# A hybrid encoder step on one core: x rows added by VectorE on the way out of PSUM, and another order of the second projections

## The chip, the cores and the metric

One core of a Trainium2 chip runs the whole program. The metric is the device time of one execution in microseconds (us); a smaller number is better. A GB/s is 10^9 bytes a second, a KB in the tables of the profile is 1024 bytes.

## The reference

One layer, with the same weights for 1024 new frames (prompt) and 32 frames of a running stream (sample), D_MODEL = 1024, float32 throughout:

```
x += concat[mLSTM(4 heads of 128), sliding-window attention(8 heads of 64)](rmsnorm(x) W_in) W_out     # W_in: 1024 x 2824
h  = rmsnorm(x)
q  = h W_q;  s1, s2 = q halves x two sets of 128 sub-keys        # 8 heads
top 16 of s1, of s2, then top 16 of their 256 sums -> 16 of 16384 experts per head and row
x += sum over 8 heads x 16 experts of  softmax(top) * gelu(u[idx] . h) * v[idx]     # u, v: rows of 1024 float32
y  = rmsnorm(x)
```

It also returns the last 128 keys and values and the final mLSTM state of both groups. Each row of x reads 128 rows of u and 128 of v, gathered by index from HBM.

## The kernel before

**Tiles and groups.** The 1056 rows are nine tiles: 0 to 7 are the prompt's, of 128 rows, and tile 8 (`SAMPLE`) has 32. Mixing a tile (projection, mLSTM, attention, output projection, norm, queries, key scores) needs the tiles before it. The expert part goes by subtiles of 32 rows: 33 subtiles q, two groups g = 2q and 2q + 1 each, 66 groups of 16 slots, so 1056 slots t = 16 g + k. A group handles 32 rows x 4 heads = 128 partitions at once, and a slot is one of their 16 experts: a u row and a v row for each partition, 512 KB each. GpSimd issues the two indirect gathers of a slot in turn (`gather_u` of the next group, `gather_v` of this one) into rings of 5 and 7 buffers. VectorE forms the dot product of u with h (L1141) and, in `weigh` (L1109), the matrix of weights of a group; TensorE multiplies the weights by the v rows (L1502) and so sums heads and experts of a subtile in the PSUM tile `acc`. Even experts go to the subtile's own 32 partitions of `acc`, odd ones to 32 others.

**Out of PSUM.** At the start of a subtile `begin_parts` (TensorE, L1462) puts the subtile's x rows into its own part of `acc`, by a product with the identity. When its 32 slots are done, `gather_parts` on ScalarE copies the other part to SBUF (L733), TensorE adds that to the own part (L1448), and ScalarE copies the own part to `xt` (L736). After the last subtile of a tile it sums the squares (L742), and `finish` on VectorE scales the rows (L1119), from where they are stored.

**What sets the order.** Every engine runs the same loop over slots, each a program of its own, in order. The mixing of tile m is woven in by the tables `PE_AT`, `ACT_AT` and `DVE_AT`: a step's name, a part and a row r, and `slot_of(m, r)` turns a row into a slot. Tiles 5 to 7 take 1.24 slots a row, tile 4 0.60, tile 3 0.60 in its second part, and the sample tile 1.06. The slot says only where in each engine's stream the step stands; semaphores do the rest, and a step that waits holds up its engine. In the tables `out_proj` (L1382) ends at row 61; `residual` (VectorE, L1028) adds its sum to x, `norm_root` (ScalarE) and `normalise` (VectorE) follow, then `h2_transpose`, sixteen `query` steps (L1397) and four `score_keys` (L1408).

**Two passes of the projection.** The weights W_in, W_out and W_q don't fit in SBUF together: W_in (six chunks of columns) shares its place `weights` with W_out and W_q. Tiles 0 to 3 (`FIRST` = 4) are projected at the start. At slot 288 (`AGAIN`) W_in comes again, and tiles 4, 5, 6, 7 and the sample are projected at slots 288 to 391: 24 slots a tile, a half chunk every second slot (`project_at`), 8 for the sample. Each chunk is scaled on its way out of PSUM to `po_again` (L581, L834, and L849 for the sample's last two) and stored to a scratch tensor in HBM (L390, L401). Then W_out (L375) and W_q in four loads of two row blocks (L366) come back. `load_p` (L333 to L336) reads a tile's rows of the projection (644, 256 and 512 KB) and of the rotation table (8 KB) before its mixing. The queue of SyncE issues all of this, in the order of its program. For tile 4 the first steps that need the rows are `gates` on VectorE (L894) and `qk_transpose` on TensorE (L1288), at slot 399.

```
def begin_parts(q):
    if q >= 2: pe.wait_ge(sub_out, q - 1)
    for half in range(2):
        T.matmul(acc[r, cols], ident[r, r], xt[m % 2][r, cols], start=True, stop=False)
```

## Time and profile before

| | |
|---|---|
| median of 3 runs | 3286.49 us (3281.36 to 3294.59) |
| the profiled execution | 3287.95 us |
| its span, first to last instruction | 3286.2 us |
| mean granted clock of TensorE | 0.84 |
| DMA | 1206.27 MB, 367 GB/s over the span |
| busy: TensorE, VectorE, GpSimd, ScalarE | 2585.3, 2079.2, 1995.7, 580.3 us |

The DMA share of a stretch is the mean busy share of the core's sixteen DMA engines; it can come out a little over 1. Records of TensorE count twice for each float32 product that the code writes: a product of 512 columns is two records. A stretch of the trace is named by its us from the start of the span.

### The profile page before, as it was taken

The numbers are of one execution on the slowest core, as the hardware profiler recorded it, in microseconds if no ns is written. First come the engines' busy times: TensorE is split into PE (matmuls) and PEld (weight loads), VectorE is DVE, ScalarE is ACT, GpSimd is POOL, SyncE is SP. The second block draws the span as 40 slices with busy tenths as digits, with TensorE's granted clock in tenths as the row PEclk, the third lists the DMA queues.
The fourth block names the chain that finished last, engine by engine and source line by source line (L and its number), as shares of the span: only waits on it lengthen the run. The fifth ranks groups of instructions, "written<-read, shape, count | busy, mean of one in ns | idle before, by whom it ended". The sixth has DMA issues, their size and how long they took to land.

```text
span 3286.2 us, 34549 instructions
## 1 busy us (share of the span) xinstructions
PE 2585.3 (79%) x11351; PEld 1055.1 (32%) x11351; DVE 2079.2 (63%) x5202; ACT 580.3 (18%) x1057; POOL 1995.7 (61%) x2128
## 2 busy tenths in 40 slices
PE   8995886788769899947967786778767886789666
PEld 4562352235224433313522242234222341125111
DVE  1246677776776467637657776777677667765653
ACT  2211111211121212112112111211122111210111
POOL 0015576767765466636567676777676676755775
PEclk9996897789788999968888897789878887775878
DMA  6079999999999999998899999999999999988998
GB/s 243 26 267 403 344 376 405 396 364 407 409 386 379 344 407 407 373 384 316 330 361 408 396 401 407 399 398 403 407 409 384 366 407 399 406 337 296 394 405 331
DMA packets 351818, 1206.27 MB, mean 367 GB/s; under 512 B 37840, under 2 KB 55128, under 8 KB 349592
## 3 DMA queue, kind: packets, MB, share of 16 engines
q0 software_dynamic: 304128, 1107.43, 86.3%
q1 hardware_dynamic: 47512, 96.64, 7.9%
q8 instruction: 91, 1.49, 0.2%
q14 instruction: 87, 0.71, 0.1%
HBM read 1188.42 MB, written 15.60 MB: 366 GB/s over the span
## 4 chain that ended last, share of the span: by engine, by line
PE 40%; DMA 23%; DVE 13%; POOL 10%; issue 6%; DVEq 4%; ACT 2%; SPq 1%; ACTq 1%; POOLq 0%
DMA ring<-in_peer_u_dram,idx 13%; PE acc L1502 12%; DMA ring<-in_peer_v_dram,idx 7%; DVE ring L1141 7%; PE mx L1397 6%; POOL ring L529 5%; POOL ring L518 5%; PE mx L1382 4%; PE acc L1213 4%; PE acc L1462 3%; PE mx L1228 3%; DVEq L1045 2%; PE h2p L1437 2%; PE acc L1448 2%; DMA proj_scratch<-weights 1%
## 5 line engine op out<-in xcount | busy, mean ns | idle before, releaser
L1502 PE MATMUL acc<-ring,wk 128*32 128x512 f32 x4224 | 1259.6, 729 | 474.8 <-DMA ring<-in_peer_v_dram,idx 436.1
L1141 DVE SCALAR_TENSOR_TENSOR ring<-ring,h2p 128x1024 f32<-128x1024 f32 x1056 | 1281.0, 1216 | 556.1 <-DMA ring<-in_peer_u_dram,idx 466.5
L518 POOL DMA_INDIRECT ring<-in_peer_u_dram,idx x1056 | 997.1, 944 | 720.5 <-DVE ring L1141 264.9
L529 POOL DMA_INDIRECT ring<-in_peer_v_dram,idx x1056 | 996.5, 944 | 550.8 <-issue 273.6
L1502 PEld LDWEIGHTS acc<-ring,wk 128*32 128x32 f32 x4224 | 252.5, 123 | 1305.6 <-issue 1233.1
L1397 PEld LDWEIGHTS mx<-reg,weights 128*128 128x128 f32 x2048 | 249.9, 202 | 73.5 <-issue 73.5
L1397 PE MATMUL mx<-reg,weights 128*128 128x128 f32 (+1 forms) x2048 | 263.7, 288 | 2.0 <-DVEq L1024 1.3
L1462 PE MATMUL acc<-xt,ident 32*32 32x512 f32 x132 | 100.1, 899 | 94.1 <-DVEq L1110 94.1
L721 ACT ACTIVATE gl<-dots 128x16 f32<-128x16 f32 x66 | 14.2, 216 | 702.7 <-DVEq L1144 702.6
L1437 PE MATMUL h2p<-ch,ident 32*32 32x512 f32 x528 | 86.3, 780 | 55.6 <-DVEq L1144 55.6
L1382 PE MATMUL mx<-weights,reg 128*128 128x512 f32 (+1 forms) x256 | 128.2, 655 | 0.0
L736 ACT COPY xt<-acc 32x1024 f32<-32x1024 f32 x33 | 33.1, 1003 | 377.0 <-PE acc L1448 377.0
L1228 PE MATMUL mx<-weights,reg 128*128 128x512 f32 (+1 forms) x192 | 85.2, 588 | 3.2 <-ACTq L569 3.2
L1141 DVE DVE_READ_ACCUMULATOR ring<-ring,h2p 128x1 f32 x1056 | 87.2, 83 | 0.0
L681 ACT COPY pj<-mx 128x512 f32<-128x512 f32 (+1 forms) x36 | 19.8, 550 | 374.7 <-PE mx L1397 374.6
L721 ACT ACT_TABLE_LOAD x66 | 84.7, 1283 | 5.6
L1228 PE MATMUL mx<-weights 128*128 128x512 f32 (+1 forms) x192 | 83.8, 580 | 0.0
L1213 PE MATMUL acc<-weights,ring 128*128 128x512 f32 (+1 forms) x192 | 79.4, 572 | 0.0
L1213 PE MATMUL acc<-weights 128*128 128x512 f32 (+1 forms) x192 | 77.5, 559 | 0.0
L1448 PE MATMUL acc<-part,ident 32*32 32x512 f32 x132 | 74.6, 690 | 1.1 <-ACTq L734 1.1
L1028 DVE TENSOR_TENSOR xt<-xt,mx 128x1024 f32<-128x1024 f32 (+1 forms) x9 | 11.0, 1220 | 100.1 <-PE mx L1382 100.1
L1382 PEld LDWEIGHTS mx<-weights,reg 128*128 128x128 f32 (+1 forms) x256 | 48.8, 197 | 74.3 <-issue 73.9
(279 smaller groups left out, 2339.6 us busy)
## 6 DMA issues: line engine op xcount, KB each, us to landing
weights<-in_w_in_dram SPq DMA_DIRECT2D x10, 2048.0 KB, 18.9
ring<-in_peer_u_dram,idx POOLq DMA_INDIRECT x1056, 8.1
ring<-in_peer_v_dram,idx POOLq DMA_INDIRECT x1056, 8.0
weights<-in_peer_w_q_dram SPq DMA_DIRECT2D x8, 2048.0 KB, 26.9
ring<-in_peer_w_q_dram SPq DMA_DIRECT2D x8, 1024.0 KB, 5.7
weights<-in_w_out_dram SPq DMA_DIRECT2D x2, 4096.0 KB, 23.5
proj_scratch<-weights SPq DMA_DIRECT2D x20, 256.0 KB, 6.1
pj<-proj_scratch SPq DMA_DIRECT2D x7, 644.0 KB, 13.9
```

Source lines behind the costliest of these rows:

```text
L518: pool.indirect_dma_start(ring[:, n % NU, :], None, u_d, bass.IndirectOffsetOnAxis(ap=idx[:, g % 4, k:k + 1], axis=0)).then_inc(u_in[n % N ...
L529: pool.indirect_dma_start(ring[:, NU + n % NV, :], None, v_d, bass.IndirectOffsetOnAxis(ap=idx[:, g % 4, k:k + 1], axis=0)).then_inc(v_in[ ...
L721: S.activation(gl[:, :], dots[:, g % 2, :], ACT.Gelu)
L1141: V.scalar_tensor_tensor(ring[:, n % NU, :], ring[:, n % NU, :], 1.0, h2p[:, :], ALU.mult, ALU.mult, accum_out=dots[:, (g + 1) % 2, k:k + ...
L1213: last = T.matmul(pbank[c], hT1[b][:, k, :], win_s[c][:, k, :], start=k == 0, stop=k == DC - 1)
L1228: last = T.matmul(pbank_again[c], hT1_again[b][:, k, :], win_s[c][:, k, :], start=k == 0, stop=k == DC - 1)
L1382: last = T.matmul(mx[0:n, 2 + half, :], t8[:, k, 0:n], w, start=k == 0, stop=k == DC - 1)
L1397: last = T.matmul(mx[:, i // 4, i % 4 * P:i % 4 * P + n], w, t8[:, k, 0:n], start=k == 0, stop=k == DC - 1)
L1437: last = T.matmul(h2p[j * SUB:(j + 1) * SUB, cols], ident[r, r], ch[m % 2][r, cols], start=True, stop=True)
L1448: last = T.matmul(acc[r, cols], ident[other, other], part[other, cols], start=False, stop=True)
L1462: T.matmul(acc[r, cols], ident[r, r], xt[m % 2][r, cols], start=True, stop=False)
L1502: last = T.matmul(acc[j:j + SUB, cols], wk[:, g % 2, i, :], ring[:, NU + (TOPK * g + i) % NV, cols], start=not own and g % 2 == 0 and i == ...
```

## The change

There are two parts.

**The x rows.** `begin_parts` no longer issues products. The first even expert of a subtile starts the sum in its own part (`start` for i < 2). ScalarE's `gather_parts` ends after the copy of the other part. A new step on VectorE, `add_rows`, stands at k = 6 of every even group, waits for TensorE's sum and adds the own part of `acc` to `xt`. The squares of a finished tile move into `square_rows` on ScalarE, at k = 7 of every eighth group. VectorE's last `finish` but one moves from k = 5 to k = 14 of its group.

**The order of the second projections.** `ORDER` makes it 5, 6, 7, sample, 4, in the same slots 288 to 391. Tile 4, which is mixed next, is scaled from PSUM straight to where the mixing reads it (`first`), as tile 0 is, and is neither stored nor read back; `load_p(4)` reads the rotation table alone. The sample's stores now stand ahead of the weights, and W_out and the four loads of W_q are issued one by one, each when a chunk of tile 4 is done. The tables change too: `residual` and what follows up to `h2_copy` start three rows later (`residual` 63 to 66), the queries two (73 to 75), the scores one (90 to 91), tile 4's slots begin six earlier (396 to 390), and tile 3's second part takes 0.56 slots a row.

```
+ORDER = [0, 1, 2, 3, 5, 6, 7, SAMPLE, FIRST]
+AT_S, AT_LAST = TILES - 2, TILES - 1
...
-PE_AT += [("out_proj", i, 58 + i // 2) for i in range(8)] + [("h2_transpose", 0, 69)]
-PE_AT += [("query", i, 73 + i) for i in range(16)] + [("score_keys", i, 90 + i) for i in range(4)]
+PE_AT += [("out_proj", i, 58 + i // 2) for i in range(8)] + [("h2_transpose", 0, 72)]
+PE_AT += [("query", i, 75 + i) for i in range(16)] + [("score_keys", i, 91 + i) for i in range(4)]
...
-        return 206 + r * 85 // 100 if r < 51 else 262 + (r - 51) * 60 // 100
+        return 206 + r * 85 // 100 if r < 51 else 263 + (r - 51) * 56 // 100
     if m == 4:
-        return 396 + r * 60 // 100
+        return 390 + r * 60 // 100
...
+    return AGAIN + 2 * (((n - FIRST) * NC_ + c) * 2 + half) - (2 * 2 * (NC_ - 2) if n == AT_LAST else 0)
...
             def load_p(m):
                 sp.wait_ge(keys_scored, m)
-                if m == FIRST:
-                    sp.wait_ge(sc_ready, m)
...
+                if m == FIRST:
+                    sp.dma_start(rot[0:n, :], rot_tab[r:r + n, :]).then_inc(p_in, 16)
+                    return
...
+                load_x1_again(AT_LAST)
+                sp.wait_ge(chunk_act, copies_until(AT_S) + 1)
...
+                for c in range(1, NC_):
+                    sp.wait_ge(chunk_ready, chunks_until(AT_LAST) + c + 1)
+                    if c == 1:
+                        load_wout()
+                    else:
+                        if c == NC_ - 1:
+                            sp.wait_ge(po_out, 16 * NC_ * (TILES - 1 - FIRST))
+                        load_wq(2 * (c - 2))
...
+                if m == AT_LAST:
+                    V.tensor_scalar(first[c], pbank_again[c], rinv, None, ALU.mult)
...
                 act.drain().then_inc(part_ready, 1)
-                act.wait_ge(sub_ready, q + 1)
-                S.copy(xt[m % 2][r, :], acc[r, :])
-                act.drain().then_inc(sub_out, 1)
...
+            def add_rows(q):
+                m, s = q // 4, q % 4
+                r = slice(s * SUB, (s + 1) * SUB)
+                dve.wait_ge(sub_ready, q + 1)
+                V.tensor_tensor(xt[m % 2][r, :], xt[m % 2][r, :], acc[r, :], ALU.add)
+                dve.drain().then_inc(sub_out, 1)
...
             def begin_parts(q):
-                for half in range(2):
-                    cols = slice(half * 512, half * 512 + 512)
-                    T.matmul(acc[r, cols], ident[r, r], xt[m % 2][r, cols], start=True, stop=False)
...
-                                                start=not own and g % 2 == 0 and i == 1, stop=not own and g % 2 == 1 and i == TOPK - 1)
+                                                start=g % 2 == 0 and i < 2, stop=not own and g % 2 == 1 and i == TOPK - 1)
```

SyncE's queue, where the second projections end and tile 4's rows are loaded (`reg` holds x rows that are projected, `weights` holds both the weights and `po_again`). Before:

```order
L390 DMA proj_scratch<-weights 128x264 [waits chunk_dve]
L375 DMA weights<-in_w_out_dram 128x8x1024 [waits chunk_ready]
L366 DMA weights<-in_peer_w_q_dram 128x2x2048 x2
L401 DMA proj_scratch<-weights 32x512 [waits chunk_act]
L401 DMA proj_scratch<-weights 32x512 x3
L366 DMA weights<-in_peer_w_q_dram 128x2x2048 [waits chunk_dve]
L401 DMA proj_scratch<-weights 32x512
L401 DMA proj_scratch<-weights 32x264
L366 DMA weights<-in_peer_w_q_dram 128x2x2048 [waits po_out]
L333 DMA pj<-proj_scratch 128x1024 [waits sc_ready,keys_scored]
L334 DMA vx<-proj_scratch 128x4x128
L335 DMA pj<-proj_scratch 128x1288
```

The same place in the changed kernel:

```order
L410 DMA proj_scratch<-weights 128x264 [waits chunk_dve]
L342 DMA reg<-in_x_prompt_dram 128x1024 [waits rms1_ready,h1_transposed]
L417 DMA proj_scratch<-weights 32x512 [waits chunk_act]
L417 DMA proj_scratch<-weights 32x512 x3
L417 DMA proj_scratch<-weights 32x512 [waits chunk_dve]
L417 DMA proj_scratch<-weights 32x264
L395 DMA weights<-in_w_out_dram 128x8x1024 [waits chunk_ready]
L386 DMA weights<-in_peer_w_q_dram 128x2x2048 [waits chunk_ready] x3
L386 DMA weights<-in_peer_w_q_dram 128x2x2048 [waits po_out,chunk_ready]
L351 DMA rot<-in_rotation_dram 128x16 [waits keys_scored]
```

The sample's six stores have moved ahead of W_out and W_q, the three reads of tile 4's projection are gone, and the rotation table stands directly behind the last load of W_q.

VectorE at slot 422 of the changed kernel, in the middle of tile 4's mixing (L1184 is the dot product of a slot, L1162 is `finish` of tile 2, L1115 a step of the top 16):

```order
L1160 RECIPROCAL yr<-yr 128x1
L1162 SCALAR_TENSOR_TENSOR xt<-xt,yr,mx 128x1024
L1184 SCALAR_TENSOR_TENSOR ring,dots<-ring,h2p 128x1024
L1152 TENSOR_TENSOR xt<-xt,acc 32x1024
L1115 MAX top<-co 128x8
L1184 SCALAR_TENSOR_TENSOR ring,dots<-ring,h2p 128x1024
```

The row L1152 is new, one for each of the 33 subtiles; the others stood in VectorE's stream before.

## Rows read from the trace of the kernel before

**Rows 1.** The page, part 1: busy time, share of the span, instructions
```profile
PE 2585.3 (79%) x11351; PEld 1055.1 (32%) x11351; DVE 2079.2 (63%) x5202; ACT 580.3 (18%) x1057; POOL 1995.7 (61%) x2128
```

**Rows 2.** The page, part 3, GpSimd's gathers: packets, MB, share of sixteen engines' span
```profile
q0 software_dynamic: 304128, 1107.43, 86.3%
```

**Rows 3.** Stretches: length, busy us of each engine, granted clock, DMA share, GB/s
```profile
271.40:3286.20 3014.80, 2341.78 (x10271) 911.49 (x10270) 1999.22 (x4963) 520.09 (x937) 1966.00 (x2083) 0.83 0.98 382
...
1396.50:1482.00 85.50, 37.70 (x159) 9.61 (x160) 28.21 (x68) 12.54 (x17) 29.69 (x32) 0.66 0.95 376
1482.00:1526.00 44.00, 31.46 (x135) 13.21 (x135) 39.98 (x120) 11.17 (x27) 30.82 (x33) 0.81 0.98 372
1526.00:1690.80 164.80, 138.85 (x773) 73.56 (x772) 92.65 (x217) 27.45 (x50) 89.28 (x95) 0.85 0.84 314
...
1593.90:1647.00 53.10, 49.53 (x335) 34.26 (x334) 40.38 (x97) 9.25 (x14) 31.06 (x33) 0.94 0.88 327
...
2501.30:2592.80 91.50, 74.36 (x273) 29.05 (x272) 61.92 (x145) 19.44 (x40) 57.61 (x62) 0.82 0.94 360
2887.20:3050.10 162.90, 148.91 (x620) 71.89 (x621) 92.86 (x227) 16.86 (x28) 89.07 (x95) 0.69 0.83 308
...
3050.10:3135.50 85.40, 50.78 (x160) 10.24 (x159) 57.53 (x142) 9.68 (x15) 64.66 (x69) 0.79 1.03 409
3254.00:3286.20 32.20, 17.18 (x68) 3.96 (x68) 1.42 (x2) 4.73 (x6) 9.87 (x11) 0.91 0.57 210
```

**Rows 4.** Groups by line: busy us, mean ns | idle before, what ended it
```profile
L1397 PE MATMUL mx<-reg,weights 128*128 128x128 f32 (+1 forms) x2048 | 263.7, 288 | 2.0 <-DVEq L1024 1.3 <-issue 0.8
L1462 PE MATMUL acc<-xt,ident 32*32 32x512 f32 x132 | 100.1, 899 | 94.1 <-DVEq L1110 94.1
...
L736 ACT COPY xt<-acc 32x1024 f32<-32x1024 f32 x33 | 33.1, 1003 | 377.0 <-PE acc L1448 377.0
...
L1028 DVE TENSOR_TENSOR xt<-xt,mx 128x1024 f32<-128x1024 f32 (+1 forms) x9 | 11.0, 1220 | 100.1 <-PE mx L1382 100.1
```

**Rows 5.** DMA issues by line: count, KB each, median us to landing
```profile
weights<-in_peer_w_q_dram SPq DMA_DIRECT2D x8, 2048.0 KB, 26.9
...
pj<-proj_scratch SPq DMA_DIRECT2D x7, 644.0 KB, 13.9
...
pj<-proj_scratch SPq DMA_DIRECT2D x7, 512.0 KB, 6.5
...
reg<-in_x_prompt_dram SPq DMA_DIRECT2D x4, 512.0 KB, 9.9
vx<-proj_scratch SPq DMA_DIRECT2D x7, 256.0 KB, 11.6
```

**Rows 6.** Waits from 1404 to 1482 us: us in total, times, longest
```profile
DVE weights L849 <- DMA proj_scratch<-weights: 33.2, 1, 33.2
...
DVE g L894 <- DMA rot<-in_rotation_dram: 16.8, 1, 16.8
...
PE mx L1288 <- DMA rot<-in_rotation_dram: 9.5, 1, 9.5
```

**Rows 7.** Chain of waits, 1500 to 1692 and 2880 to 3052 us: start, us, what
```profile
1522.46 3.62 PE acc L1462 x4
...
1645.23 1.83 PE acc L1462 x4
...
2942.53 3.44 PE acc L1462 x4
```

**Rows 8.** Timeline of TensorE at 1608 and at 2995 us: start, us, instruction
```profile
1608.24 3.84 PE L1397 MATMUL mx<-reg,weights 128*128 128x128 f32 x32
1612.01 1.91 PE L1502 MATMUL acc<-ring,wk 128*32 128x512 f32 x8
...
2995.32 3.63 PE L1502 MATMUL acc<-ring,wk 128*32 128x512 f32 x8
2998.88 7.04 PE L1397 MATMUL mx<-reg,weights 128*128 128x32 f32 x32
```

More of the change, by code:

```diff
@@ L106, in keep_at, with project_at, chunks_until, copies_until @@
     return 8 * TOPK * m - 52
-def project_at(m, c, half):
-    return AGAIN + 2 * (((m - FIRST) * NC_ + c) * 2 + half)
+def project_at(n, c, half):
+    return AGAIN + 2 * (((n - FIRST) * NC_ + c) * 2 + half) - (2 * 2 * (NC_ - 2) if n == AT_LAST else 0)
+def chunks_until(n):
+    return NC_ * n if n <= AT_S else NC_ * (n - 1) + 2
+def copies_until(n):
+    return 3 * n if n <= AT_S else 3 * (n - 1) + 1
+def p_landed(m):
+    return 64 * m if m < FIRST else 64 * (m - 1) + 16
 def by_slot(table):
@@ L766, in _ @@
                         gather_parts(g // 2 - 1)
+                    if k == 7 and g > 0 and g % 8 == 0:
+                        square_rows(g // 2 - 1)
                     if g < 0 and k in LAST_ACT:
@@ L781, in _ @@
                         hT1_copy(FIRST)
-                    for m in range(FIRST, TILES):
-                        if m < SAMPLE and t == project_at(m, 1, 0):
-                            rms1(m + 1)
-                        if m < SAMPLE and t == project_at(m, 4, 0) + 1:
-                            hT1_copy(m + 1)
-                        for c in range(0, NC_ if m < SAMPLE else 1, 2):
-                            if t == project_at(m, c, 1) + 1:
-                                chunk_copy(m, c)
+                    for n in range(FIRST, TILES):
+                        if n < AT_LAST and t == project_at(n, 1, 0):
+                            rms1(n + 1)
+                        if n < AT_LAST and t == project_at(n, 4 if n < AT_S else 1, 0) + 1:
+                            hT1_copy(n + 1)
+                        for c in range(0, NC_ if n != AT_S else 1, 2):
+                            if t == project_at(n, c, 1) + 1:
+                                chunk_copy(n, c)
                     if t == window(SAMPLE) + 2:
@@ L1146, in _ @@
                         weigh(g)
-                    if k == 5 and g == 8 * SAMPLE:
+                    if k == 6 and g > 0 and g % 2 == 0:
+                        add_rows(g // 2 - 1)
+                    if k == 14 and g == 8 * SAMPLE:
                         finish(SAMPLE - 1)
@@ L1509, in _ @@
                         transpose1(FIRST)
-                    for m in range(FIRST, TILES):
-                        for c in range(NC_ if m < SAMPLE else 2):
+                    for n in range(FIRST, TILES):
+                        for c in range(NC_ if n != AT_S else 2):
                             for half in range(2):
-                                if t == project_at(m, c, half):
-                                    if c == 4 and half == 0:
-                                        transpose1(m + 1)
-                                    project_again(m, c, half)
+                                if t == project_at(n, c, half):
+                                    if n < AT_LAST and c == (4 if n < AT_S else 1) and half == 0:
+                                        transpose1(n + 1)
+                                    project_again(n, c, half)
                     if t == window(SAMPLE) + 1:
```

106 lines of the change are left out of this document (56 added, 50 removed).

## The prediction

> **What bounds the kernel now.** I read the busy times first [rows 1]: TensorE is busy 79% of the span, VectorE 63%, GpSimd 61%, so none of them is the bound over the whole. The DMA queues come next: the expert gathers of GpSimd alone move 1107 MB and take 86.3% of sixteen engines' span [rows 2]. Then the stretches, which say where that bound holds [rows 3]. The reader is to see three kinds. From 3050 to 3136 us the DMA share is 1.03 at 409 GB/s with TensorE busy 51 of 85 us: gathers come as fast as they can, and nothing that another engine gains or loses there moves the end. I take 409 as the full rate. Over all that follows the first gathers (271 to 3286 us) the mean is 382, so 3014.8 x (409 - 382)/409 = 199 us are lost against full rate. Only those can be won, besides bytes. By the same formula the other rows hold: 6.9 us in 1396 to 1482 (tile 4 waits for its rows), 4.0 in 1482 to 1526, 38.3 in 1526 to 1691 (tile 4 is mixed in 60 slots, where others have 120), 11.0 in 2501 to 2593 (output projection of tile 7), 40.2 in 2887 to 3050 (the sample tile) and 15.7 in the tail, in all 116. The other 83 us are spread over short stretches.
>
> **The products of the x rows.** L1462 goes: 132 records, 100.1 us of TensorE [rows 4], 3.03 us for each of 33 subtiles (132 are four each). It looks like 3% of the time, but counts only where TensorE is late. On the chain of waits three of its 33 places lie in the two dense stretches: 3.62, 1.83 and 3.44 us [rows 7], 8.9 us together. The other 30 lie mostly where gathers run at full rate and cost nothing now; some begin the short losses. Their ends are 0 and 25 us (the 91 us of TensorE time that is left, at the share of 83 us lost in about 3000); I take 4, near the bottom, since VectorE's weights end the wait just as often as TensorE does.
>
> **The copy that becomes an addition.** ScalarE's L736 (33.1 us, 1003 ns each) goes, and so does its wait of 377.0 us in all for L1448 [rows 4], 11.4 us at the start of every second group in which ScalarE's mixing steps stood still. ScalarE is busy 18%, so this is worth what lies behind it on the chain: I take 1 us, ends 0 and 6. VectorE gets 33 additions of 32x1024 from PSUM. The nearest row is L1028, the same operation and length, 11.0 us for 9, so 1.22 us each and 40 us in all. They stand six slots into the group, four slots behind TensorE's gather_parts, so that VectorE rarely waits. In full-rate stretches they are covered by the wait for gathers; in the dense ones three of them and one wait of a few us for a late TensorE remain (near 1646 us VectorE reaches that slot some 4 us before TensorE has done L1448; at the 31 other places that I compared it comes later than TensorE): minus 4 us, ends minus 12 and 0. In the tail 1.22 replaces 1.00 with one more change of engine: minus 0.4.
>
> **The residual three rows later.** L1028 waits 100.1 us in all for the output projection, 11 us a tile [rows 4], and stands before VectorE's dot products. Starting it three rows later (3 to 4 slots, in tile 4 under two) lets those go first. But the same TensorE backlog delays the expert products anyway. Worth plus 2, ends 0 and 12.
>
> **Tile 4 projected last.** Its projection was stored and read back: 644 + 512 + 256 = 1412 KB in, as much out [rows 5], 2.89 MB in all. At 409 GB/s that is 7.1 us, and as DMA is the bound it counts in full. No product is added or lost: tiles 5, 6, 7, sample and 4 take the same slots, 288 to 391. The waits change. Now VectorE waits 33.2 us in L849 for stores that are queued behind 8 MB of weights, then 16.8 us for the rotation table behind the last weights and tile 4's rows, and TensorE 9.5 us for the same [rows 6]. Most of this is covered by the weight traffic itself (376 GB/s, only 6.9 + 4.0 us lost). After the change the sample's stores go ahead of any weight load, so L849's wait goes; the weights are then issued one by one as chunks of tile 4 are done. What stays: 8 KB of rotation table still stand behind the last query weights, issued when TensorE has done the last chunk, and the first mixing step of tile 4 on VectorE waits for them. I expect 10 to 20 us there, covered by 2 MB of weights and up to 12 gathers in flight of 0.5 MB (8 MB, 20 us at full rate). New is also a near wait: the x rows of tile 4 are fetched some four slots (11 us) before they are transposed, and such a load lands in 9.9 us [rows 5]; late by a few us at most, under the same cover. So the transition gives plus 4, ends minus 15 and plus 11. Mixing begins 6 slots earlier at the same density, so the dense stretch moves and does not shrink.
>
> The weight load against the gathers is where a rule bears. The median load of 2 MB of query weights takes 26.9 us to land [rows 5], with several queued at once; four slots between them are about 11 us. The Trainium skill (DMA: Bandwidth & Descriptors, Queues, rings and completion order) says that each DMA engine takes turns between the queues that have work, packet by packet. By that rule the weights would get no more than about half the rate while gathers are pending, the table would land late, and the sum would be that of the second rival below.
>
> **Sum.** 7.1 + 4 + 8.9 + 4 + 1 + 2 - 4 - 0.4 = 22.6 us. The profiled execution took 3287.95 us (span 3286.2 and 1.75 around it), so 3265.4; the median of the runs shown is 1.5 lower, 3286.49, so **3264 us**.
>
> **Rivals.**
> *Bytes only.* The cover is better than I think: TensorE's 100 us and the waits all lie beside gathers, a gain in a dense stretch is lost to the next late engine (the softmax, the norm root), and 7.1 us remain: 3279. For it: 0.98 mean DMA share in the whole stretch [rows 3]. Against: L1462 stands on the chain just where the share is 0.84.
> *The transition gives back.* Weights (4 MB and four times 2 MB in 16 slots, some 42 us) at half of 409 GB/s need 61 us, so the table lands 20 us later than I assume, VectorE stands still for 35 us, and its cover of 20 us is used up: minus 15 in place of plus 4, so 3264 + 19 = 3283. For it: a wait of 33 us there in the trace of before. Against: most of 4 MB goes out early.
> *Slower: the clock.* The queries of tile 4 run at 3.84 us per 32 records and expert products at 1.91 per 8; in the sample tile, whose queries have 32 columns in place of 128, the granted clock is 0.69 and 32 records take 7.04 and the products 3.63, though TensorE is busy 149 of 163 us [rows 8, 3]. That is 1.2 in place of 2.4 GHz. Taking away the products with which each second group begins leaves TensorE idle there while it waits for the weights. If tile 4's 256 query records (2048 for eight tiles [rows 4]) fell to the lower level: 256/32 x 3.2 = 26 us, and ten pairs of expert products x 1.7 = 17, together 43 on the chain: 3307. It decides from some 40 us on, so only if nearly the whole query part (1594 to 1647 us) is at 1.2 GHz. Against: the granted clock is 0.94 from 1594 to 1647 us [rows 3], and the queries are unchanged. The Trainium skill (TensorE: Matmul & The Clock Gate, Part 1) says that the engine is throttled by default and activity releases it; that is the rule that speaks against removing work from TensorE.
> That the change does nothing is no rival: the records and bytes go in any case.
>
> **Numbers.** The measurement of this kernel tells 0.5% (16.4 us) from no change, so faster means below 3270. My forecast, a gain of over 16 us: 0.60. Bytes only: 0.20, transition: 0.10, both within 0.5%. The clock: 0.10, slower. Low end: 7.1 + 11 + 8.9 + 15 + 4 + 4 - 4 = 46, near 3240, with most open terms near but not all at their best. High end 3290, where the first two rivals lie inside and the third outside. So 3240 to 3290, and 0.60, 0.30, 0.10.
>
> **What would show it.** Right: 2.9 MB less in the direct queue; no proj_scratch read for tile 4; no wait of 30 us before the sample's copy; a wait under 20 us for the rotation table; PE busy about 100 us lower, with most of it turned into idle time; the rate in the dense stretch of tile 4 above 314 GB/s and its length down by 6 to 10 us; groups outside still at 406 to 409. Wrong: a wait of over 25 us for the table with the DMA share under 0.9 beside it; the add waiting for gather_parts more than 10 us in all in the dense stretches; a granted clock under 0.8 during tile 4's queries; or a dense stretch that shrinks by over 15 us, which would mean that I sized the residual's wait or the 30 other products too low.

## The result and the profile after

| | before | after |
|---|---|---|
| median | 3290.54 us (3281.36 to 3313.73, 4 runs) | 3242.14 us (3237.88 to 3245.92, 4 runs) |
| ratio of the times | | 0.9842, 95% interval 0.9814 to 0.9870 |
| the profiled execution, its span | 3287.95, 3286.2 us | 3237.88, 3236.0 us |
| mean granted clock | 0.84 | 0.855 |
| DMA | 1206.27 MB, 367 GB/s | 1203.36 MB, 372 GB/s |

The changed kernel is 48 us faster by the medians, 1.6% (1.3 to 1.9%). I forecast 3264 us, a gain of 22.6: the side was right, the time lies just inside the range, and the size is less than half of what came. The profiled execution of before stands near the fast end of its runs, that of after at the fast end of its own, so the two profiles (50 us apart) can be set side by side.

The page of the changed kernel, parts 1 and 3, which answer to [rows 1, 2]:

```profile
PE 2490.0 (77%) x11219; PEld 1030.6 (32%) x11219; DVE 2120.2 (66%) x5235; ACT 552.5 (17%) x1028; POOL 1992.7 (62%) x2128
...
q0 software_dynamic: 304128, 1107.43, 87.4%
q1 hardware_dynamic: 45832, 93.74, 7.8%
```

TensorE has 132 records and 95 us less, VectorE 41 us more, ScalarE 28 less. The gathers are the same 1107 MB. The direct queue moves 93.74 MB; 2.9 MB less, as forecast.

Groups by line of the changed kernel, VectorE (answers to [rows 4]); idle time before, and what ended it, at the end:

```profile
L1152 DVE TENSOR_TENSOR xt<-xt,acc 32x1024 f32<-32x1024 f32 x33 | 40.1, 1216 | 27.1 <-PE acc L1498 26.3
L1063 DVE TENSOR_TENSOR xt<-xt,mx 128x1024 f32<-128x1024 f32 (+1 forms) x9 | 11.0, 1217 | 34.4 <-PE mx L1432 33.8 <-issue 0.6
```

The addition costs 1216 ns, as the estimate from L1028 said, and never waits for TensorE except at the very end of the kernel (26.3 us, one wait, the tail). The residual's wait for the output projection fell from 100.1 to 33.8 us.

Stretches of the changed kernel, with the columns of [rows 3]: the end of the weight loads, tile 4 beginning, tile 4 mixed, its query part, output projection of tile 7, the sample tile, and a free stretch behind it:

```profile
1398.60:1459.00 60.40, 41.28 (x154) 14.94 (x154) 33.44 (x85) 11.61 (x20) 29.89 (x32) 0.78 1.00 402
1459.00:1505.40 46.40, 30.98 (x117) 12.25 (x117) 37.12 (x98) 15.33 (x39) 29.23 (x32) 0.79 0.91 332
1505.40:1656.90 151.50, 124.23 (x744) 63.98 (x744) 95.50 (x226) 21.23 (x33) 90.81 (x97) 0.87 0.92 342
1561.30:1612.30 51.00, 50.30 (x457) 37.73 (x461) 32.01 (x84) 6.12 (x10) 28.47 (x31) 0.95 0.90 326
2462.90:2547.80 84.90, 72.50 (x270) 28.22 (x272) 63.57 (x150) 15.70 (x29) 58.32 (x62) 0.80 1.01 398
2846.70:3002.10 155.40, 135.02 (x613) 67.60 (x613) 91.79 (x219) 14.96 (x27) 90.22 (x96) 0.76 0.88 327
3002.10:3086.00 83.90, 50.74 (x161) 10.63 (x161) 60.70 (x153) 12.43 (x19) 62.85 (x67) 0.79 1.03 406
```

The full rate is still 406 to 409. Tile 4's dense part took 151.5 us at 342 GB/s in place of 164.8 at 314, the sample tile 155.4 at 327 in place of 162.9 at 308. To see where all the time went I put the formula of the prediction (length x (409 - GB/s)/409) on each of the 66 groups, cut where TensorE's first expert product of a group starts, and summed. Lost against full rate, in us:

| groups | before | after | what is there |
|---|---|---|---|
| 24 to 28 | 49.2 | 34.7 | tile 4 begins and is mixed densely |
| 57 to 59 | 40.0 | 31.1 | the sample tile |
| 27 even groups from 4 to 64 | 46.8 | 25.0 | a subtile starts, mixing at normal density |
| 26 odd groups from 5 to 63 | 28.1 | 31.5 | a subtile's second half |
| 0 to 3, 65 | 34.8 | 30.0 | start and tail |
| all | 198.9 | 152.4 | |

Less by 46.5 us, and 7.1 us of bytes, in one execution of each. The largest part, 21.8 us, went where I had put the least: the even groups, those that begin with L1462.

Of the two waits of VectorE in tile 4's transition one is gone and one is shorter. SyncE's timeline from 1355 us, and the DMA issues from 1355 to 1425 us (KB each, median us to landing):

```profile
1358.29 0.40 SPq L395 DMA_DIRECT2D weights<-in_w_out_dram  x1
1369.23 46.69 SPq L386 DMA_DIRECT2D weights<-in_peer_w_q_dram  x4
1415.97 0.47 SPq L351 DMA_DIRECT2D rot<-in_rotation_dram  x1
```

```profile
q0 software_dynamic: 4578, 16.66, 59.7%
q1 hardware_dynamic: 2065, 12.20, 42.4%
...
weights<-in_peer_w_q_dram SPq DMA_DIRECT2D x4, 2048.0 KB, 15.1
weights<-in_w_out_dram SPq DMA_DIRECT2D x1, 4096.0 KB, 25.0
...
rot<-in_rotation_dram SPq DMA_DIRECT2D x1, 8.0 KB, 13.4
```

The table of rotations landed 13.4 us after its issue, and VectorE's waits from 1390 to 1460 us hold none for it, where [rows 6] had 16.8:

```profile
DVE ring L1184 <- DMA ring<-in_peer_u_dram,idx: 20.7, 11, 5.3
DVE ea L958 <- PE mx L1362: 5.1, 1, 5.1
DVE ring L1184 <- PE h2p L1487: 3.8, 1, 3.8
```

The sample's copy (now L882) stands before that, at 1335 us. Its wait is down from 33.2 us to this (waits from 1250 to 1460 us):

```profile
DVE weights L882 <- remote: 9.0, 1, 9.0
```

"remote" means that this trace doesn't name what ended it. The same wait is 9.0 us in f1 and 8.7 in i1 below, ended there by TensorE.

### The profile page after: what moved, and what is told of

Its sections match the earlier page's. It is cut to its first block, busy times and chain, and to the rows that moved or that the text cites. A ratio compares the mean times of both kernels' runs of the same rounds, so it can differ in the third digit from the quotient of the medians.

```text
span 3236.0 us, 34286 instructions
## 1 busy us (share of the span) xinstructions
PE 2490.0 (77%) x11219; PEld 1030.6 (32%) x11219; DVE 2120.2 (66%) x5235; ACT 552.5 (17%) x1028; POOL 1992.7 (62%) x2128
## 2 busy tenths in 40 slices
DMA packets 350136, 1203.36 MB, mean 372 GB/s; under 512 B 37696, under 2 KB 54344, under 8 KB 347912
## 3 DMA queue, kind: packets, MB, share of 16 engines
q1 hardware_dynamic: 45832, 93.74, 7.8%
## 4 chain that ended last, share of the span: by engine, by line
PE 33%; DMA 28%; POOL 14%; DVE 12%; issue 7%; DVEq 4%; SPq 1%; ACT 0%; another core or an unknown queue 0%; ACTq 0%; POOLq 0%
DMA ring<-in_peer_u_dram,idx 17%; PE acc L1547 10%; DMA ring<-in_peer_v_dram,idx 9%; POOL ring L551 7%; POOL ring L540 7%; PE mx L1447 6%; DVE ring L1184 6%; PE acc L1259 4%; PE mx L1432 3%; PE mx L1274 3%; PE h2p L1487 2%; DVEq L1080 2%; PE mx L1389 1%; DMA proj_scratch<-ring 1%; DVEq L1139 1%
## 5 line engine op out<-in xcount | busy, mean ns | idle before, releaser
L1547 PE MATMUL acc<-ring,wk 128*32 128x512 f32 x4224 | 1272.5, 735 | 657.2 <-DMA ring<-in_peer_v_dram,idx 534.4
L1184 DVE SCALAR_TENSOR_TENSOR ring<-ring,h2p 128x1024 f32<-128x1024 f32 x1056 | 1283.1, 1216 | 622.8 <-DMA ring<-in_peer_u_dram,idx 528.9
L1274 PE MATMUL mx<-weights,reg 128*128 128x512 f32 (+1 forms) x288 | 125.7, 580 | 3.1 <-ACTq L591 3.1
L1432 PE MATMUL mx<-weights,reg 128*128 128x512 f32 (+1 forms) x256 | 122.4, 631 | 0.0
L1184 DVE DVE_READ_ACCUMULATOR ring<-ring,h2p 128x1 f32 x1056 | 86.9, 82 | 0.0
L1498 PE MATMUL acc<-part,ident 32*32 32x512 f32 x132 | 83.4, 762 | 3.3 <-ACTq L760 3.3
L1274 PEld LDWEIGHTS mx<-weights,reg 128*128 128x128 f32 x288 | 52.7, 193 | 77.6 <-issue 73.0
L1152 DVE TENSOR_TENSOR xt<-xt,acc 32x1024 f32<-32x1024 f32 x33 | 40.1, 1216 | 27.1 <-PE acc L1498 26.3
L1127 DVE TENSOR_TENSOR co<-co,i2f 128x256 f32<-128x256 f32 x132 | 50.6, 424 | 6.4 <-issue 0.4
```

The lines of the kernel that those rows point to most:

```text
L1184: V.scalar_tensor_tensor(ring[:, n % NU, :], ring[:, n % NU, :], 1.0, h2p[:, :], ALU.mult, ALU.mult, accum_out=dots[:, (g + 1) % 2, k:k + ...
L1274: last = T.matmul(pbank_again[c], hT1_again[b][:, k, :], win_s[c][:, k, :], start=k == 0, stop=k == DC - 1)
L1432: last = T.matmul(mx[0:n, 2 + half, :], t8[:, k, 0:n], w, start=k == 0, stop=k == DC - 1)
L1498: last = T.matmul(acc[r, cols], ident[other, other], part[other, cols], start=False, stop=True)
L1547: last = T.matmul(acc[j:j + SUB, cols], wk[:, g % 2, i, :], ring[:, NU + (TOPK * g + i) % NV, cols], start=g % 2 == 0 and i < 2, stop=not ...
```

## The experiments

The experiments came in five sets, e to i. The letters of the theories don't mean the same in all of them. In set e and in f1's text, **A** says that the residual's later row was sized too low, **B** that the products of x rows and the blocked ScalarE were, **C** that tile 4's transition was. From set g on, **A** is the prediction's view: TensorE is late in the dense stretches, and the products of x rows count there. **B** there says that they count at nearly every subtile start, by a few us each. In the expectations "the changed kernel" and "the kernel before" are the two of this text. Ratios are to the kernel before in the same set, with 95% intervals. In sets e and h all kernels, the one before too, took 9 to 10% longer, so ratios are compared, not us. Code is shortened: `...` stands for what is left out, and a line such as `DVE_AT: (...)` names entries of a table and is not the line itself.

### The change taken apart

e1_rows: the kernel before with the part on the x rows alone.

```
-                act.wait_ge(sub_ready, q + 1)
-                S.copy(xt[m % 2][r, :], acc[r, :])
...
+                    if k == 6 and g > 0 and g % 2 == 0:
+                        add_rows(g // 2 - 1)
...
-                    T.matmul(acc[r, cols], ident[r, r], xt[m % 2][r, cols], start=True, stop=False)
```

> The kernel before with the x rows added by VectorE alone (no products of the x rows, ScalarE's second copy gone, add_rows at k = 6, square_rows at k = 7); tables and order of projections as before. The prediction's own terms give a gain of 8.9 + 4 + 1 - 4 - 0.4 = 9.5 us for this. Theory A (the later residual was sized too low): 8 to 14 us, since this part was sized about right. Theory B (the products and the blocked ScalarE were sized too low): 25 to 35 us, with the dense stretch of tile 4 and the stretch of the sample tile shorter by 8 us or more each.

e2_order: the kernel before with ORDER and all that follows from it; tables and slots stay.

```
+ORDER = [0, 1, 2, 3, 5, 6, 7, SAMPLE, FIRST]
...
         return 396 + r * 60 // 100
```

> The kernel before with the new order of the second projections alone (tile 4 last, straight from PSUM; weights one by one); products and tables as before, tile 4 still begins at slot 396. The prediction's terms give 7.1 + 4 = 11 us. Theories A and B: 8 to 14 us. Theory C (the transition was sized too low): 20 us or more, with little lost DMA time left between slots 384 and 416.

e3_tables: the kernel before with the rows of the tables alone.

```
-DVE_AT: ("residual", 0, 63), ("normalise", 0, 67), ("h2_copy", 0, 71)
+DVE_AT: ("residual", 0, 66), ("normalise", 0, 70), ("h2_copy", 0, 74)
-PE_AT: ("h2_transpose", 0, 69), ("query", i, 73 + i), ("score_keys", i, 90 + i)
+PE_AT: ("h2_transpose", 0, 72), ("query", i, 75 + i), ("score_keys", i, 91 + i)
```

> The kernel before with the rows of the tables alone (residual and its followers three rows later, queries two, scores one); the products and the order of projections as before. The prediction gives 2 us. Theory A: 12 to 20 us, and VectorE's wait of 100 us for the output projection falls under 50. Theories B and C: 0 to 4 us, since a TensorE that is late delays the expert products in any case.

e4_after_old_tables: the changed kernel with the old tables and old slots of tiles 3 and 4.

```
-        return 390 + r * 60 // 100
+        return 396 + r * 60 // 100
...
-DVE_AT: ("residual", 0, 66)
+DVE_AT: ("residual", 0, 63)
```

> The changed kernel with the old tables and the old slots of tiles 3 and 4; products gone, tile 4 projected last. Against the kernel before: by the prediction's terms a gain of 20.6 us; by theory A 20 to 25 us (so 25 us slower than the changed kernel); by theory B 40 to 46 us (close to the changed kernel's gain of 48); by theory C 30 to 40 us.

| | median us | ratio | interval |
|---|---|---|---|
| before, there | 3591.41 | | |
| e1_rows | 3562.54 | 0.9914 | 0.9889 to 0.9940 |
| e2_order | 3574.06 | 0.9941 | 0.9915 to 0.9967 |
| e3_tables | 3582.61 | 0.9985 | 0.9959 to 1.0011 |
| e4_after_old_tables | 3554.59 | 0.9889 | 0.9861 to 0.9918 |

The x rows alone bring 0.9% where my terms for them (8.9 + 4 + 1 - 4 - 0.4 = 9.5 us) are 0.3%; that is B's size. The order brings 0.6%, 21 us there, where I had 11.1 us, 0.3%; that is C's size, though the interval begins at 0.33%, inside what A and B expected. The tables alone can't be told from nothing, though the wait that they were to shorten went from 100.1 us to this (groups by line of e3_tables):

```profile
L1028 DVE TENSOR_TENSOR xt<-xt,mx 128x1024 f32<-128x1024 f32 (+1 forms) x9 | 11.0, 1219 | 40.2 <-PE mx L1382 39.6 <-issue 0.6
```

60 us of idle time gone and no gain to be measured: in the kernel before that wait was beside other waits. In the changed kernel it may be otherwise: e4, without the new tables and slots, stands at 0.9889, and the changed kernel in three sets at 0.9827 to 0.9843. The two are some 0.5% apart (0.2 to 0.9% by the intervals).

### The products, the copy, the residual

f1_after_again: the changed kernel once more; here the kernel before takes about what it took in the first set.

> The changed kernel itself, beside the kernel before on the same chip as the parts below. If the parts simply added up (rows 0.86%, order 0.59%, tables 0.15% in the runs above) the ratio is 0.984. Against rows and order without the tables (0.9889 above) theory A expects 0.984 or less, so that the tables give 0.5% or 15 us in the changed kernel; if the tables give no more here than alone, 0.987 to 0.989.

f2_copy_on_dve: the kernel before; products stay, the copy out of `acc` moves from ScalarE to VectorE at k = 6.

```
-                S.copy(xt[m % 2][r, :], acc[r, :])
...
+                V.tensor_copy(xt[m % 2][r, :], acc[r, :])
```

> The kernel before, its products of the x rows kept, but the copy out of acc made by VectorE (a copy at k = 6 in place of the addition) and not by ScalarE. It has the relief of ScalarE and the load on VectorE, and none of the relief of TensorE. If TensorE's products are what counts: ratio 0.998 to 1.003. If the blocked ScalarE was what counted: 0.991 to 0.994, most of the gain of the x rows.

f3_no_product: the kernel before without the products, so that x is missing from the sum; ScalarE's copy stays.

```
-                    T.matmul(acc[r, cols], ident[r, r], xt[m % 2][r, cols], start=True, stop=False)
...
-                                                start=not own and g % 2 == 0 and i == 1, ...
+                                                start=g % 2 == 0 and i < 2, ...
```

> The kernel before without the products of the x rows, ScalarE's copy kept; x is not added to the expert sum here, so y lacks it. It has TensorE's relief alone. If the products are what counts: ratio 0.990 to 0.993 (25 to 35 us on this chip, where before takes 3590). By the prediction's terms 8.9 + 4 = 13 us, ratio 0.996.

f4_residual_early: the changed kernel with `residual` alone back at row 63.

```
-("residual", 0, 66), ("normalise", 0, 70)
+("residual", 0, 63), ("normalise", 0, 70)
```

> The changed kernel with the residual back at row 63 (norm_root, normalise and everything behind stay at their new rows). If the wait of VectorE for the output projection is what the tables remove: 0.3 to 0.5% slower than the changed kernel (ratio 0.988), with L1063 waiting some 100 us again. If the later queries are what matters, or neither: equal to the changed kernel within 0.15%.

| | median us | ratio | interval |
|---|---|---|---|
| before, there | 3300.18 | | |
| f1_after_again | 3242.85 | 0.9827 | 0.9801 to 0.9854 |
| f2_copy_on_dve | 3285.59 | 0.9961 | 0.9934 to 0.9987 |
| f3_no_product | 3260.87 | 0.9876 | 0.9850 to 0.9901 |
| f4_residual_early | 3251.39 | 0.9861 | 0.9835 to 0.9888 |

Leaving the products out brings 1.2% by itself, 41 us, three times my 8.9 + 4 and more than either case of its text. By the groups, f3's loss in 24 to 28 is 45.6 (49.2 before), in 57 to 59 37.6 (40.0), in the 27 even groups 24.6 (46.8): the dense stretches hardly move, the even groups give 22 us. They count at the subtile starts.

f4 is 8.5 us slower than f1. The intervals of their ratios touch, but both hold the spread of the same kernel before; side by side on one chip the slowest of f1's five runs took 3246.53 us and the fastest of f4's five 3248.59. By the means the residual's row is worth some 4 to 17 us in the changed kernel. Its wait for the output projection, which is 37.1 us in f1, has grown again (groups by line of f4):

```profile
L1063 DVE TENSOR_TENSOR xt<-xt,mx 128x1024 f32<-128x1024 f32 (+1 forms) x9 | 11.0, 1220 | 83.4 <-PE mx L1432 83.4
```

f2 lies between the two cases of its text: a gain of 0.1 to 0.7%. Its profile shows none (202.5 us lost in all, 198.9 before), but that execution was one of its slower ones (3292.24 us, median 3285.59). So the copy stays open here.

### Where the products cost: three, thirty, twice

g1_double_product: each product issued twice.

```
+                    for again in range(2):
-                    T.matmul(acc[r, cols], ..., start=True, stop=False)
+                        T.matmul(acc[r, cols], ..., start=True, stop=again == 0)
```

> The kernel before, with each product of the x rows issued twice into the same place (the second one starts the sum again, so the output is the same): 100 us of TensorE more, spread over 33 subtile starts, nothing else changed. Theory A (TensorE is late only in the two dense stretches, 1526 to 1691 and 2887 to 3050 us, as I forecast): only three or four of the 33 doubled pairs count, 9 to 15 us slower, ratio 1.003 to 1.005. Theory B (TensorE is late by a few us at many subtile starts at the normal density too, above all beside output projections and queries): about as much as removing them gave, or more, 25 to 45 us slower, ratio 1.008 to 1.014.

g2_three_gone and g3_thirty_gone: the products left out for three subtiles, and for the other thirty; x is missing from the sum there.

```
+DENSE = (13, 14, 29)
...
+                if q not in DENSE:        # g3: if q in DENSE
                     for half in range(2):
...
```

> The kernel before without the products of three subtiles only (13, 14 and 29, the three whose products stood on the chain of waits in the dense stretches); y lacks the x rows in these three subtiles, so 3 of 33 x 3.03 us of TensorE go. My term for them was 8.9 us. Theory A: 9 to 15 us faster, ratio 0.995 to 0.997, most of what can be had from the products. Theory B: 5 to 9 us, ratio 0.997 to 0.999, a small part of it. Loss against full rate in groups 26 to 28 down from 38 to 30 to 33 us, the groups outside as before.

> The kernel before without the products of the other thirty subtiles; y lacks the x rows there. My term for them was 4 us, with ends 0 and 25. Theory A: 0 to 6 us faster, ratio 0.998 to 1.000. Theory B (the short losses of the groups outside the dense stretches are TensorE's): 15 to 32 us faster, ratio 0.990 to 0.9955; losses of groups 8, 9, 16, 32, 38 and 48 to 50 together down from 37 us to under 20, groups 26 to 28 near 38 as before.

g4_order_tables: the changed kernel with the part on the x rows undone.

```
-                    if k == 6 and g > 0 and g % 2 == 0:
-                        add_rows(g // 2 - 1)
...
+                    T.matmul(acc[r, cols], ident[r, r], xt[m % 2][r, cols], start=True, stop=False)
```

> The changed kernel with the part on the x rows undone: products of the x rows by TensorE and ScalarE's copies are back, the new order, the tables and the slots of tiles 3 and 4 stay. If the parts add up (x rows worth 27 to 31 us, order with tables the rest of 48 us): 3268 to 3275 us, ratio 0.993 to 0.995. Rival, that the parts need each other (without TensorE's relief the earlier slots of tile 4 only move its backlog): 3280 or more, ratio over 0.997.

| | median us | ratio | interval | even groups lose |
|---|---|---|---|---|
| before, there | 3293.32 | | | 46.8 us |
| g1_double_product | 3382.00 | 1.0277 | 1.0233 to 1.0320 | 125.3 |
| g2_three_gone | 3291.56 | 1.0003 | 0.9979 to 1.0028 | 56.0 |
| g3_thirty_gone | 3265.21 | 0.9923 | 0.9899 to 0.9946 | 27.7 |
| g4_order_tables | 3267.69 | 0.9924 | 0.9895 to 0.9953 | 53.4 |

This turns my two terms round. The three products that stood on the chain [rows 7], priced at 8.9 us, are worth nothing by themselves (at most 0.2%, 7 us). The thirty that I let cost 4 are worth 25 us (18 to 33). Doubling missed both expectations: 99 us of TensorE more cost 89, nine tenths of it, where leaving out thirty pairs (91 us) returned 25 and all of them 41. So in the kernel before a subtile start has hardly any spare time, and the cost bends there: nothing more fits in, and what is taken out soon returns no more. One thing stays open: three and thirty left out bring 25 us together, all thirty-three 41 (33 to 50, f3 in another set). Either the three are worth something once the thirty are gone, or the sets differ by more than their intervals say; no run tells.

The two parts of the change add up: e1's ratio times g4's is 0.9914 x 0.9924 = 0.9839, and the changed kernel measured 0.9827 to 0.9843. Order and tables bring 0.76%. The x rows bring the rest, 0.9843/0.9924 (the first number is i1's, below), 0.8% or 27 us (11 to 43 by the two intervals).

Why no spare time? TensorE at the start of group 44, in the kernel before and in g1:

```profile
2320.40 1.10 PE L1408 MATMUL mx<-kT,pj 128*32 128x128 f32 x28
2324.85 3.56 PE L1462 MATMUL acc<-xt,ident 32*32 32x512 f32 x4 [3.36 <-DVEq L1110]
2328.34 3.59 PE L1502 MATMUL acc<-ring,wk 128*32 128x512 f32 x8
```

```profile
2385.50 1.10 PE L1408 MATMUL mx<-kT,pj 128*32 128x128 f32 x28
2389.99 7.03 PE L1463 MATMUL acc<-xt,ident 32*32 32x512 f32 x8 [3.40 <-DVEq L1110]
2396.95 3.63 PE L1503 MATMUL acc<-ring,wk 128*32 128x512 f32 x8
```

And GpSimd at the same places, before and g1, where it issues the gather of the next v rows:

```profile
2328.50 0.94 POOL L518 DMA_INDIRECT ring<-in_peer_u_dram,idx  x1 [0.30 <-issue]
2332.20 0.94 POOL L529 DMA_INDIRECT ring<-in_peer_v_dram,idx  x1 [2.77 <-PE acc L1502]
```

```profile
2393.85 0.94 POOL L518 DMA_INDIRECT ring<-in_peer_u_dram,idx  x1 [0.31 <-issue]
2400.85 0.94 POOL L529 DMA_INDIRECT ring<-in_peer_v_dram,idx  x1 [6.07 <-PE acc L1503]
```

The reader is to see one chain. TensorE has nothing to do for 3.36 us, until VectorE's weights come (L1110). Only then do the products of x rows start, and only behind them the first expert products, which free v buffers. GpSimd, with seven of them, waits 2.77 us for the first. In the kernel before the DMA queues just outlast that: 404 GB/s over the 16 us behind it, 407 over 44. In g1 the wait is 3.3 us longer, and the 16 us behind it run at 351 GB/s. Before, then g1:

```profile
2328.00:2344.00 16.00, 12.17 (x69) 3.21 (x68) 10.63 (x27) 2.69 (x4) 10.18 (x12) 0.88 1.03 404
2328.00:2372.00 44.00, 27.84 (x117) 6.01 (x116) 25.73 (x58) 7.33 (x8) 28.28 (x31) 0.73 1.03 407
```

```profile
2397.00:2413.00 16.00, 12.52 (x69) 3.82 (x68) 7.96 (x20) 2.69 (x4) 8.87 (x10) 0.82 0.91 351
```

Over the whole kernel the 27 even groups lose 78.5 us more in g1 than before (125.3 and 46.8), 2.9 us each: nearly the length of the added products. GpSimd's waits for a free v buffer, before and g1 (us in total, times, longest), grow by 103 us:

```profile
POOL ring L529 <- PE acc L1502: 252.7, 154, 9.7
```

```profile
POOL ring L529 <- PE acc L1503: 356.1, 156, 9.4
```

In f3, without the products, they are 199.1 us.

### Work or place

That made a third question: is it TensorE's work, or its place behind the wait for the weights? h1_products_early exchanges two statements of the kernel before, with the same 132 records; h2_double_early does so with doubled products; h3_after_products_early is g4 with the exchange.

```
-                            pe.wait_ge(wk_ready, g + 1)
                             if g % 2 == 0:
                                 begin_parts(g // 2)
+                            pe.wait_ge(wk_ready, g + 1)
```

> The kernel before with one pair of lines exchanged: the products of the x rows are issued before TensorE waits for VectorE's weights and not after it. The same work (132 records, 100 us). Theory P (the place is what costs: they lie on the way from VectorE's weights to the first v buffer that comes free; before them TensorE idles 94.1 us in 33 places, 2.85 us each against 3.03 us of products): nearly the whole gain of leaving them out, 20 to 35 us faster, ratio 0.989 to 0.994, and the loss of the 27 even groups outside the dense stretches down from 46.8 us to 25 to 32. Theory W (TensorE's work itself is what is late): within 6 us of before, ratio 0.998 to 1.002.

> As h1, but with each product issued twice: 200 us of TensorE, of which some 2.85 us a subtile fit in the idle time ahead of the weights and some 3 to 4 us don't. Theory P: about the time of the kernel before, 0 to 15 us slower, ratio 1.000 to 1.005. Theory W: as the doubled products behind the wait, 80 to 100 us slower, ratio 1.024 to 1.030.

> The changed kernel without its part on the x rows (products by TensorE and copies by ScalarE, as in g4), but with the products ahead of the wait for the weights. Theory P: as fast as the changed kernel, 3238 to 3250 us, ratio 0.982 to 0.987; faster than it if VectorE's 40 us of additions cost something. Theory W: as g4, 3265 to 3272 us, ratio 0.991 to 0.994.

| | median us | ratio | interval |
|---|---|---|---|
| before, there | 3633.70 | | |
| h1_products_early | 3607.74 | 0.9929 | 0.9900 to 0.9957 |
| h2_double_early | 3629.08 | 0.9991 | 0.9972 to 1.0010 |
| h3_after_products_early | 3583.13 | 0.9845 | 0.9817 to 0.9872 |

It is the place. The same products ahead of the wait bring 0.7%, about what leaving thirty of them out brought; W, which expected next to nothing in h1, 2.4 to 3.0% slower in h2 and 0.991 or more in h3, is outside all three intervals. The doubled products of h2 take the time of the kernel before, which has them once. That doesn't mean that the second pair was free: h2 is 21 us slower than h1 (9 to 31). But behind the wait the second pair cost 89. The difference is what fits into TensorE's idle time. Of the 33 starts 25 have some, 94.1 us together [rows 4], so 3.8 us on the mean; the texts of h1 and h2 spread it over all 33. h2's products take 155.3 us, 4.7 a start.

With the place comes a second thing, which was not tried by itself: TensorE has worked just before, and a record of these products takes 723 ns in h1 and 899 in the kernel before.

(The losses of groups that h1's text names aren't read, since the rate in this set was lower than 409 nearly throughout.) Last, the changed kernel and h3's kernel side by side where the kernel before took what it took in the first set:

> The changed kernel itself, beside i2 on one chip. Both theories of the x rows expect it where it was, a ratio of 0.981 to 0.988 on a chip like the first; on a slower one a little nearer to 1.

> The kernel of h3: the changed kernel with products by TensorE ahead of the wait for weights and copies by ScalarE in place of VectorE's additions. If only the place of the products counted and VectorE's additions are covered: the same as i1 within 0.3%. If the additions cost what I took for them (4 us and more): 4 to 12 us faster than i1. If ScalarE's copies, which wait for TensorE at the start of every second group, still cost something: 5 to 15 us slower than i1.

i1 took 3242.45 us, ratio 0.9843 (0.9805 to 0.9881), i2 3237.65 us, ratio 0.9832 (0.9789 to 0.9876), before 3293.62. The same within what can be told (some 0.4% either way, six runs each): products by TensorE in the right place are about as good as VectorE's additions. i2 beats the kernel before, but not the changed one. TensorE at the start of group 44 in i2:

```profile
2294.28 1.10 PE L1443 MATMUL mx<-kT,pj 128*32 128x128 f32 x28
2295.31 1.90 PE L1497 MATMUL acc<-xt,ident 32*32 32x512 f32 x4
2297.14 1.05 PE L1537 MATMUL acc<-ring,wk 128*32 128x512 f32 x4
```

The products run straight behind the scores, at 1.90 us and not 3.56; the engine has not idled before them, and before the 3.56 it had, for 3.36 us. Over all subtiles (groups by line of i2, to be set beside L1462 of [rows 4]):

```profile
L1497 PE MATMUL acc<-xt,ident 32*32 32x512 f32 x132 | 69.8, 651 | 3.5 <-DVEq L870 3.5
```

## Why the prediction was right and wrong

**Right.** Bytes: 2.9 MB less, no read of tile 4's projection. The wait of the sample's copy is 9.0 us and not 33.2, and the table of rotations held nobody up. VectorE's additions cost 1216 ns each and wait for nothing inside the loop. The full rate is unchanged. The clock rival did not come: in tile 4's query part the granted clock is 0.95 (0.94 before), and the mean rose. The second rival (weights at half rate hold the table back) did not come either: with W_out on its way first, the four loads of query weights landed in 15.1 us by the median, where [rows 5] had 26.9 for all eight. The gathers held 59.7% of the DMA engines' time and the direct queue 42.4% meanwhile; so sharing by turns, as the Trainium skill (DMA: Bandwidth & Descriptors, Queues, rings and completion order) has it, is not contradicted, but it did no harm.

**The step that failed** is "The other 30 lie mostly where gathers run at full rate and cost nothing now [...] I take 4". g3 measured 25 us for them, and g2 nothing for the three that I priced from the chain at 8.9. That 25 is also the upper end that I gave is luck: the working beside it, 91 us at a share of 83 in about 3000, is 2.5 us and not 25, so the bound had no ground, and by the right sum it would have been far too low.

The cause of the first error is this. I read the full rate of a stretch as spare time of TensorE. But full rate in the kernel before meant only that GpSimd's wait for the v buffer ended just in time (2.77 us at 2332). In other groups and executions it ends a little late: the profiled one of before lost 46.8 us in the 27 even groups, those of g4 and g2, which have the same products there, 53.4 and 56.0. And the row that told it was in my own group 4: `94.1 <-DVEq L1110` is idle time just before L1462, in 25 of its 33 places; so the product stands on the way from VectorE's weights to the first free v buffer. I used it only to argue that the weights end the wait as often as TensorE does. Right, but what follows behind the weights is then in full on that path. In the dense stretches it is otherwise: g2 shows that three products that stand on the chain can go for nothing. My reading is that TensorE has a backlog of queries there, so that other work takes the place of what is removed, and that the chain does not show what lies close beside it; no run tried that by itself.

**Sizes, part by part.** The x rows: forecast 9.5, measured 27 (g4 against i1, 11 to 43) and 0.9% alone (e1), 28 us of 3290. Order and tables: forecast 7.1 + 4 + 2 = 13.1, measured 25 us (g4: 0.9895 to 0.9953, 15 to 35 us). Of that step the sentence "the dense stretch moves and does not shrink" was wrong: groups 24 to 28 lose 41.1 us in g4 and 49.2 before (46.3 in g2, which has the old order too, one execution each). The groups name where: group 28 lost 8.6 us before and 5.5 in g2, and 0.5 in g4, since mixing that starts six slots earlier is done when it begins, and the start lies beside the weight loads at 402 GB/s. That this is the reason was not tried by itself. A further part is the residual's row, 8.5 us in the changed kernel (f4) where the sum had 2. The rest is not placed: the sample tile's groups differ between executions of kernels that are alike there (10 to 25 us in group 59, below).

**The copy, the addition and the residual.** I had 1 for ScalarE's relief, minus 4 for the additions, plus 2 for the residual. i1 against i2, whose products are early, puts the first two together at minus 0.5 to plus 0.2%, by the medians' difference of 5 us and the spread of the runs. f2 hints at a gain from the copy (0.1 to 0.7%) with no trace of it in its profile. f3 against e1, 0.9876 and 0.9914, hints that the additions cost up to 0.4% or 12 us; the intervals overlap. These two stay unsettled within some 16 us. The residual's 60 us of shorter wait are worth 0.15% or nothing in the kernel before (e3), and 8.5 us (4 to 17) in the changed one (f4).

All of it together was 48, 57 and 51 us by the medians of the three sets. I said that a dense stretch shrinking by over 15 us would mean that the 30 products were sized too low. They were, but it shrank by 13; the even groups were the place to look.

## What to carry to other kernels

Where a producer, a ring of buffers and a consumer run in step, price work by where it stands against the wait that the ring ends on, and not by the rate around it: the same 100 us of TensorE cost some 26 us more behind the wait for the weights than ahead of it, and a second 100 us cost 89 behind it and 21 ahead. Before work is moved to another engine, look at the idle time just in front of it ("idle before, and what ended it"); if the work doesn't need what that wait is for, exchange the two lines first. A stretch at full rate can be without a reserve: doubling the disputed work in an experiment measures the reserve, which leaving it out does not.

## What the runs showed that I had not expected

**A steadier time.** All 61 runs of the kernel before outside sets e and h lie between 3270.24 and 3322.00 us, the 15 of the changed kernel between 3231.72 and 3247.55. An explanation would be that with no reserve at subtile starts small differences in landing times add up. It was not tested, and i2 speaks against it: its products are out of the way too, and its six runs lie between 3222.53 and 3252.93.

**Clock and rate in one group.** Group 59, the queries of the sample tile, in the changed kernel and in i2:

```profile
2939.70:3002.10 62.40, 61.89 (x290) 39.19 (x289) 23.29 (x53) 4.33 (x10) 27.30 (x29) 0.60 0.73 243
```

```profile
2951.90:3000.30 48.40, 48.02 (x295) 27.85 (x296) 24.44 (x60) 5.25 (x10) 28.68 (x31) 0.82 0.91 324
```

The same work with TensorE busy throughout takes 62.4 us at a granted clock of 0.60 and 48.4 at 0.82: 14 us in one place, in one execution each. The Trainium skill (TensorE: Matmul & The Clock Gate, Part 1) says that the default is throttled and activity releases it; the 1.90 and 3.56 us of the same four records above agree, but this group doesn't fit: TensorE was busy for 61.9 of 62.4 us, and the mean was 0.60. It isn't i2's code that decides, or not alone: the same kernel as h3 took 61.0 us for this group at 0.64, and e4, with VectorE's additions, 43.6 us at 0.77. What decides stays open.

**Slower sets.** In the sets e and h the kernel before takes 3591 and 3634 us in place of 3290. From 600 to 3400 us their kernels move 344 to 352 GB/s; the kernel before has 382 behind its first gathers in the first set. Whether that is the chip isn't shown: set e (3591 us) and set f (3300) ran on a chip of the same number, 0, and set h on number 5. In the row of TensorE's expert products of h1, 134.6 us of the idle time are ended by "issue", which the row of the expert products has in none of the faster sets:

```profile
L1502 PE MATMUL acc<-ring,wk 128*32 128x512 f32 x4224 | 1336.4, 754 | 634.0 <-DMA ring<-in_peer_v_dram,idx 392.2 <-issue 134.6 <-DVEq L1110 105.5
```

The ratios there (h3 0.9845) agree with that of a faster set for the same kernel (i2 0.9832).
